# A feed-forward in two phases, with the down product as seven block products

## The reference, cut to what matters

```python
def swiglu(x, w_gate, w_up, w_down):
    return (jax.nn.silu(x @ w_gate) * (x @ w_up)) @ w_down
```

## Time and profile before

| what | value |
|---|---|
| median of 3 timed runs | 1898.8 us (1897.58 to 1910.72) |
| span of the profiled execution, first to last instruction | 1893.8 us |
| TensorE busy | 1788.9 us |
| VectorE busy | 843.5 us |
| ScalarE busy | 413.6 us |
| GpSimd busy | 57.5 us |
| read from memory | 230.07 MB |

### The profile page before, as it was taken

How to read it: one execution, slowest core, us unless ns; L and a number is a source line. 1 busy time by engine, 2 the same in 40 slices (tenths; PEclk the granted TensorE clock), 3 DMA queues, 4 the chain that set the end, 5 groups by cost and what they waited for, 6 DMA issues and landing times.

```text
span 1893.8 us, 25538 instructions
## 1 busy us (share of the span) xinstructions
PE 1788.9 (94%) x10478; PEld 1358.7 (72%) x10478; DVE 843.5 (45%) x1790; ACT 413.6 (22%) x1010; POOL 57.5 (3%) x71
## 2 busy tenths in 40 slices
PE   7999989999999999999988999899998999999997
PEld 5777768776587876878766778587886677556774
DVE  3244333744334335444357747434433444324353
ACT  1000022533200002000146412200002253113521
POOL 0200000000000000000003130000000000000000
PEclk9999998999999999999998959999998999999999
DMA  6754554212344544544433300254556762467520
GB/s 225 251 181 142 137 134 134 67 67 81 120 156 136 198 134 134 177 157 161 158 103 105 126 24 1 90 162 150 168 157 102 114 96 84 88 82 106 99 89 22
DMA packets 194168, 232.74 MB, mean 123 GB/s; under 512 B 27028, under 2 KB 175960, under 8 KB 194056
## 3 DMA queue, kind: packets, MB, share of 16 engines
q1 hardware_dynamic: 191584, 224.97, 43.3%
q0 software_dynamic: 1840, 5.12, 0.9%
q10 hardware_dynamic: 632, 1.04, 0.1%
HBM read 230.07 MB, written 1.05 MB: 122 GB/s over the span
## 4 chain that ended last, share of the span: by engine, by line
PE 89%; DVE 5%; ACT 2%; issue 2%; DMA 1%; ACTq 0%; DVEq 0%
PE ps L502 26%; PE ps L275 25%; PE ps L555 15%; PE ps L462 6%; PE ps L516 3%; PE ps L1629 1%; DMA ring<-in_ffn_w_up 1%; PE ps L1464 1%; PE ps L358 1%; PE ps L2148 1%; PE ps L2164 1%; PE ps L2152 1%; PE ps L2178 1%; PE ps L2183 1%; PE ps L1646 1%
## 5 line engine op out<-in xcount | busy, mean ns | idle before, releaser
L275 PE MATMUL ps<-hT,ring 128*128 128x272 f32 (+2 forms) x1504 | 363.9, 396 | 3.6 <-issue 1.3
L275 PEld LDWEIGHTS ps<-hT,ring 128*128 128x128 f32 (+1 forms) x1504 | 280.8, 190 | 65.2 <-issue 8.5
L555 PE MATMUL ps<-ring,arena 128*128 128x512 f32 x704 | 309.4, 592 | 0.0
L555 PEld LDWEIGHTS ps<-ring,arena 128*128 128x128 f32 x704 | 130.4, 190 | 147.3 <-issue 147.3
L502 PE MATMUL ps<-arena 128*128 128x128 f32 x1920 | 222.7, 276 | 0.0
L502 PEld LDWEIGHTS ps<-arena 128*128 128x128 f32 x1920 | 219.4, 193 | 0.0
L502 PEld LDWEIGHTS ps<-hT,ring 128*128 128x128 f32 x1280 | 156.8, 193 | 26.0 <-issue 19.1
L502 PE MATMUL ps<-hT,ring 128*128 128x128 f32 x1280 | 163.6, 276 | 6.4 <-DMA ring<-in_ffn_w_up 6.4
L627 DVE TENSOR_TENSOR arena<-arena,ps 128x256 f32<-128x256 f32 x40 | 16.8, 421 | 256.5 <-ACT arena L591 256.5
L640 DVE TENSOR_TENSOR arena<-arena,ps 128x384 f32<-128x384 f32 x80 | 44.2, 554 | 183.4 <-PE ps L502 183.4
L593 ACT ACTIVATE arena<-arena 128x512 f32<-128x512 f32 x40 | 25.2, 630 | 384.7 <-DVE arena L640 384.7
(11 more groups left out here) (408 smaller groups left out, 2165.7 us busy)
## 6 DMA issues: line engine op xcount, KB each, us to landing
ring<-in_ffn_w_gate SPq DMA_DIRECT2D x44, 1024.0 KB, 5.5
ring<-in_ffn_w_up SPq DMA_DIRECT2D x44, 1024.0 KB, 5.8
ring<-in_ffn_w_down SPq DMA_DIRECT2D x44, 1024.0 KB, 5.0
ring<-in_w_in SPq DMA_DIRECT2D x32, 1024.0 KB, 9.4
ring<-in_ab_w_in SPq DMA_DIRECT2D x12, 1024.0 KB, 5.3
ring<-in_w_out SPq DMA_DIRECT2D x8, 1024.0 KB, 5.0
ring<-in_ab_w_out SPq DMA_DIRECT2D x6, 1024.0 KB, 4.9
ring<-in_c_w_k SPq DMA_DIRECT2D x4, 1024.0 KB, 5.5
```

What stands on the lines that cost most here:

```text
L275: last = nc.tensor.matmul(o, l, r, start=(i == 0), stop=(i == len(pairs) - 1))
L555: m = nc.tensor.matmul(ps[:, 2 * t + h, :], hid[:, q % 2, i, t * P:(t + 1) * P], slot2(s0 + 3 * q + 2)[:, i, h * 512:(h + 1) * 512], start ...
```

## The change

The order of a feed-forward is now: gate and up of all 11 pairs, with all of `hid` kept in `arena` (11 x 512 columns), then the down product of all pairs. `plan_weights` lists all gate and up pieces first, then the 11 down pieces, and SP's loop is written out.

The down product of a pair is itself formed of seven block products, p1 to p7, of 128x512 each, gathered over the pairs in seven PSUM banks. VectorE makes four sums of weight blocks for every pair (`down_sums`) and four sums of blocks of `hid` for every four pairs (`hidden_sums`). Gate and up alternate between banks 4 to 7 and 0 to 3.

Behind it, VectorE adds the seven products to the four blocks of `y` (`y_blk`), Pool multiplies them by the gain (`trans_pool`), and ScalarE squares them from SBUF. Pool's clears for the mixer now wait for `x_new` and not for `hidden`.

```diff
         for q in range(NPAIR):
             plan.append([wide(g, 256 * q)])
             plan.append([wide(u, 256 * q)])
+        for q in range(NPAIR):
             plan.append([tall(dn, 2 * q)])
...
+            if post == 0.5:
+                c = dve_c()
+                p1, u2, u3, u4 = (y_part[:, i] for i in range(4))
...
+                dve.wait_ge(p1_out, c)
+                with_product(u2, p1, "p6").then_inc(y_step, 1)
+                with_product(y_blk[:, 0, 0], p1, "p2").then_inc(y_blk_in, 1)
+                dve.wait_ge(y_step, 3 * c - 2)
+                with_product(u4, u2, "p5").then_inc(y_step, 1)
+                dve.wait_ge(y_step, 3 * c - 1)
+                with_product(y_blk[:, 0, 1], u4, "p3").then_inc(y_blk_in, 1)
+                with_product(u3, u2, "p7").then_inc(y_step, 1)
+                dve.wait_ge(y_step, 3 * c)
+                with_product(y_blk[:, 1, 1], u3, "p5").then_inc(y_blk_in, 1)
+                with_product(y_blk[:, 1, 0], u3, "p4", ALU.subtract).then_inc(y_blk_in, 1)
+                for t in range(T):
+                    dve.wait_ge(y_sq, 2 * dve_sq())
+                    nc.vector.tensor_tensor(y_ms[:, t:t + 1], y_ss[:, 2 * t:2 * t + 1], y_ss[:, 2 * t + 1:2 * t + 2], ALU.add).then_inc(y_ms_in, 1)
+                    dve.wait_ge(y_root, dve_yr())
+                    dlink(dve, nc.vector.reciprocal(y_ms[:, t:t + 1], y_ms[:, t:t + 1]))
+                    dve.wait_ge(z_pool, 2 * dve_z())
+                    nc.vector.scalar_tensor_tensor(x[:, t, :], xn[:, t, :], y_ms[:, t:t + 1], x[:, t, :], ALU.mult, ALU.add).then_inc(x_new, 1)
...
+        def trans_pool(pool, gain):
+
+            for t in range(T):
+                for i in range(2):
+                    h = i if t == 0 else 1 - i
+                    c = slice(512 * h, 512 * h + 512)
+                    pool.wait_ge(y_blk_in, pool_b())
+                    nc.gpsimd.tensor_tensor(xn[:, t, c], y_blk[:, t, h], gains[:, gain, c], ALU.mult).then_inc(z_pool, 1)
...
+        P_BANK = {"p1": 4, "p6": 5, "p2": 6, "p5": 7, "p3": 0, "p7": 1, "p4": 2}
...
             def first_half(q):
-                n, u = s0 + 3 * q, 10 * call + q - 1
-                pe.wait_ge(a_taken, u)
+                n, u = s0 + 2 * q, 10 * call + q - 1
+                a = gu_a(q)
+                if q >= 3:
+                    pe.wait_ge(a_taken, u - 1)
...
+            def down(q):
+                slot, g, at_g = slot2(d0 + q), q // 4, q % 4
+                ts, ss = d_sum[:, q % 2], hid_sum[g][:, :, at_g]
+                sums_t, sums_s = 4 * (NPAIR * call + q), 4 * (3 * call + g)
...
+                take_slot(pe, d0 + q)
+                pe.wait_ge(hidden, c0 + q + 1)
+                if q == 0:
+                    pe.wait_ge(b_taken, 20 * call + 18)
+                m = one("p1", hid[:, q, 0, 0, :], slot[:, 0, 0:512])
...
+                pe.wait_ge(d_sums, sums_t + 3)
+                pe.wait_ge(hid_sums, sums_s + 3)
+                one("p6", ss[:, 1], ts[:, 1])
+                one("p2", hid[:, q, 1, 0, :], slot[:, 1, 0:512])
+                one("p5", ss[:, 0], ts[:, 0])
+                pe.wait_ge(hid_sums, sums_s + 4)
...
+                one("p3", ss[:, 3], slot[:, 1, 512:1024])
+                one("p7", ss[:, 2], ts[:, 2])
+                pe.wait_ge(d_sums, sums_t + 4)
+                if q == 0:
+                    pe.wait_ge(b_taken, 20 * call + 20)
+                m = one("p4", hid[:, q, 1, 1, :], ts[:, 3])
...
             direct()
             for q in range(1, NPAIR):
                 first_half(q)
...
+                second_half(q)
+            for q in range(NPAIR):
+                down(q)
...
                 if q < LAST:
                     weight_sums(dve, call, q + 1)
+                else:
+                    down_sums(dve, call, 0)
+                    down_sums(dve, call, 1)
...
+                if q == LAST - 1:
+                    hidden_sums(dve, call, 0)
+            hidden_sums(dve, call, 1)
+            for q in range(2, NPAIR):
+                down_sums(dve, call, q)
+                if q == 4:
+                    hidden_sums(dve, call, 2)
```

More of the change, by code:

```diff
@@ L304, in load_slot @@
                 sp.dma_start(dst, src).then_inc(slot_in[n % NSLOT], 16)
[L306 to L329, removed]
+        XN, SQ, XMN, SQM = arena[:, 16384:18432], arena[:, 0:1024], arena[0:META, 14336:15360], arena[0:META, 13312:14336]
         xn = XN.rearrange("p (t n) -> p t n", t=T)
@@ L533, in first_half @@
                         pe.wait_ge(w_sums, 8 * u + 2 * v + w + 1)
-                        first, m = product(gu_a[:, w, i], w_diff[:, q % 2, w, v], h_diff[:, v])
+                        first, m = product(a[:, w, i], w_diff[:, q % 2, w, v], h_diff[:, v])
                 m.then_inc(gu_half, 1)
             def second_half(q):
-                n, u = s0 + 3 * q, 10 * call + q - 1
+                n, u = s0 + 2 * q, 10 * call + q - 1
+                b = gu_b(q)
                 pe.wait_ge(h_sums, 4 * call + 4)
@@ L541, in second_half @@
                     pe.wait_ge(hidden, c0 + q)
-                else:
-                    pe.wait_ge(b_taken, 2 * u)
+                elif q >= 3:
+                    pe.wait_ge(b_taken, 2 * (u - 1))
                 for w in range(2):
-                    first, m = product(gu_b[:, w, 0], w_part(n + w, 0, 1), h_part(1, 0))
-                    if w == 1 and q < LAST:
+                    first, m = product(b[:, w, 0], w_part(n + w, 0, 1), h_part(1, 0))
+                    if w == 1:
                         first.then_inc(slot_used, 1)
@@ L548, in second_half, with one @@
                     pe.wait_ge(w_sums, 8 * u + 7 + w)
-                    product(gu_b[:, w, 1], w_diff[:, q % 2, w, 3], h_part(1, 1))
-                    first, m = product(gu_b[:, w, 2], w_part(n + w, 1, 1), h_diff[:, 3])
+                    product(b[:, w, 1], w_diff[:, q % 2, w, 3], h_part(1, 1))
+                    first, m = product(b[:, w, 2], w_part(n + w, 1, 1), h_diff[:, 3])
                     m.then_inc(gu_done, 1)
[L553 to L558, removed]
+            def down(q):
+                slot, g, at_g = slot2(d0 + q), q // 4, q % 4
+                ts, ss = d_sum[:, q % 2], hid_sum[g][:, :, at_g]
+                sums_t, sums_s = 4 * (NPAIR * call + q), 4 * (3 * call + g)
+                def one(name, left, right):
+                    m = nc.tensor.matmul(ps[:, P_BANK[name], :], left, right, start=(q == 0), stop=(q == LAST))
+                    if q == LAST:
+                        m.then_inc(p_done, 1)
+                    return m
+                take_slot(pe, d0 + q)
[4 more added lines that the diff above has]
+                if q == 0:
+                    m.then_inc(slot_used, 1)
+                pe.wait_ge(d_sums, sums_t + 3)
[4 more added lines that the diff above has]
+                pe.wait_ge(hid_sums, sums_s + 4)
+                if q == 0:
+                    pe.wait_ge(a_taken, 10 * call + 10)
+                one("p3", ss[:, 3], slot[:, 1, 512:1024])
+                one("p7", ss[:, 2], ts[:, 2])
+                pe.wait_ge(d_sums, sums_t + 4)
+                if q == 0:
+                    pe.wait_ge(b_taken, 20 * call + 20)
+                m = one("p4", hid[:, q, 1, 1, :], ts[:, 3])
+                if q < LAST:
+                    m.then_inc(slot_used, 1)
+                else:
+                    pe.drain().then_inc(slot_used, 1)
@@ L595, in weight_sums @@
         def weight_sums(dve, call, q):
-            n = at[("ffn", call)] + 3 * q
+            n = at[("ffn", call)] + 2 * q
             d_q = w_diff[:, q % 2]
@@ L1349, in mixer_pool @@
         def mixer_pool(pool):
-            pool.wait_ge(hidden, NPAIR)
+            pool.wait_ge(x_new, T)
             nc.gpsimd.memset(xpad[:, :, 0:3], 0.0).then_inc(m_zero, 1)
```

120 lines of the change are left out of this document (76 added, 44 removed).

## The result

The changed kernel takes **1880.3 us** (median of four runs, 1878.8 to 1882.1); the kernel before, beside it, takes 1898.6 (four runs). The ratio is 0.990 with a 95% interval of 0.986 to 0.993: faster, by 18 us. The forecast was 1861.6, with a range of 1850 to 1874. The direction was right, the size was half of what was forecast, and the time lies outside the range. It also lies, by 0.5 us, inside the band of 1% (1879.8 to 1917.8) that the prediction called hard to tell from no change and gave a chance of 0.06.

A forecast was written before the change was run, and what follows sets the result against it. The prediction took TensorE, busy 1788.9 of 1893.8 us, as the bound; -37.8 (down product) - 9.4 (stall) + 10.0 (ends) = -37.2 gave span 1856.6, plus 5.0 for the median, 1861.6 us; own range 1855 to 1868, with rivals 1850 to 1874.

The forecast's parts named there:

- Sum: Whole kernel: -37.8 - 9.4 + 10.0 = -37.2, span 1893.8 to 1856.6, plus 5.0 of median above span, 1861.6 us.
- Rival D: Ends of calls: longer TensorE gap, then records longer at half clock, up to 2.5 us more a call; 1871.6, chance 0.08.
- Part 1: Down product: seven matmuls a pair in place of eight, 44 pairs x 0.859 = 37.8 us less on TensorE.
- Part 2 and 3: Gate and up without the down product between them, and the border of the phases: VectorE's sums in time, cost 0.
- Part 4: Call 0: TensorE's stall for up weights goes as the ring runs three pairs ahead, 9.4 us less.
- rival B: Call 0: the stall for weights stays, 6.4 us and the clock after; -27.8, 1871.0 us, chance 0.13.
- Part 5: End of each call: longer chain of combinations, gain and x updates, 2.5 us times four, +10.0, ends 5.9 and 11.2.
- The 1.5 us of order: End of a call: row block 0 finished only after the combinations, transposes at E+5.95 instead of 4.48, four times +5.9.
- the lock: End of a call: VectorE's x update and Pool's multiplications exclude each other on SBUF; end costs 2.2 or 2.8, not 1.5.
- E: Down product: waits show at 308 single matmuls in changing banks, 0.1 us each, +31, 1892 us; chance 0.04.
- F: Gate and up: the ring starves the first phase, a pair takes 13.6, +44, time 1905.6 us; chance 0.05.
- C: Ends of calls: no exclusion between VectorE and Pool, the end costs 1.5; -41.3, 1857.5 us, chance 0.08.

The follow-up runs named there:

- b_wait1: The kernel before, with one VectorE clear of 128x1024 (about 0.9 us) put behind feed-forward call 2: 1922.8 us, one run.
- b_burst6: The kernel before, with six extra 128x512 matmuls, their result overwritten, just ahead of layer 1's recurrence: 1905.2 us, ten runs, ratio 1.000.

## Why the prediction was wrong, by its own steps

**The step that failed is the Sum**, where the span 1893.8 "becomes 1856.6" by terms of the feed-forward and its ends alone. It took for granted that all other stages keep their time. In place of nothing, the recurrence of layer 1 gave +19.9 us, all of it granted clock: 0.94 on average before, 0.50 after (19.3 over the whole stretch between the calls). The mixer of layer 0 gave another +2.6, of which 2.1 are the 32 records at a lower clock behind call 0. No rival held the 19.9. Rival D had records at half clock "up to 2.5 more a call", a small cost right behind the gap, and the 2.1 are of that kind, once and not four times; the clock that mattered failed to rise in a stage that begins some 180 us behind the end of call 2 and whose start the change had only shifted. The terms as measured, -37.8 - 9.4 + 10.8 + 2.6 + 19.3 = -14.5, make the span 1879.3, and it is 1879.4. On top the prediction put the 5.0 us by which the median of before lay above its profiled span; after, the median lies 0.9 above. That is an error of 4.1 the other way, so the span was missed by 22.8 us and the time by 18.7.

The trace of before held a warning: TensorE came to that stage at 0.50 and rose 3 us into it, in a stretch of 28.7 us that costs 48.6 if it does not rise. That stood as a possible +20 in a forecast whose whole gain was 37. The executions of the kernel before bear on it too: beside the last experiments five of 19 took 1919.8 to 1922.9 us at a mean clock of 0.952 to 0.954, all others but one 1895.6 to 1900.1 at about 0.965. That they lost the same 20 us in the same place is argued from size and clock; they left no trace. The trace of b_wait1, with the same time (1922.8) and mean clock (0.951), does show it there.

**Part 1, the down product, -37.8: held.** 66.1 us a call were foreseen (77 of these matmuls at 0.859), and the chain's piece of 65.25 for 152 records has the same 0.429 us each.

**Part 2 and 3, gate and up without cover, and the border, 0: held.** The pair takes 12.51 as before, and no window of a call holds over 0.1 us of idle TensorE. VectorE's spare time was enough for 34 us more work a call (88.8 to 123 busy).

**Part 4, the stall, -9.4: held, with less room than stated.** The load that decides was foreseen between 88.5 and 95.7; it was asked for at 68.82 and landed 24.2 us later, at 93.0. Need was put at 94.3 for TensorE and about 91 for VectorE, which did wait 1.85 us. The 5.8 us of slack that spoke against rival B was really 1.3 at TensorE (94.3 - 93.0). Pool's start was foreseen at 56.8 and was 56.60.

**Part 5, the ends, +10.0: the size held, the mechanism in part.** The four ends cost +3.05 and three times +2.6, 10.8 in all. The 1.5 us of order stood: 2.60 of gap, less the 0.69 and 0.45 that follow, is 1.46. (One reading under it was wrong: in the earlier trace rows the second multiplication, L412, waits for ScalarE's squaring and not for L410, so these rows did not show the spacing of dependent operations; the combinations end at E+1.2 as foreseen all the same.) Of the lock the prediction saw the x update (+0.45), and missed the addition of two sums of squares (+0.69), which starts while the third Pool multiplication runs. The Trainium skill, "SBUF — State Buffer", section "Who interferes with whom", covers both, since it speaks of any VectorE instruction with two SBUF inputs, and the trace agrees (0.84 against 0.15, 1.73 against 1.28); the prediction applied it only to the wide one. The end of call 0 has 0.44 more: Pool's three clears lie beside VectorE's scaling, which takes 1.19 us in place of 0.75. The prediction had put that at "at most 0.5".

**The rivals.** B, E and F did not occur. C (no lock, 1857.5) falls by the rows at the end of call 1. D's 1871.6 came nearest in number: its mechanism showed once, behind call 0, for 2.1 of the 22.8 us by which the span was missed.

## What to carry to other kernels

A change that shifts a stage by some us can turn the granted clock of a stage that it does not touch: before summing, look through the clock of every stage, and price at both levels each one that enters at 0.50. When a result disagrees with a sum whose terms all show up in the trace, put a delay of a few us and a short run of wide matmuls ahead of the suspect stage into both kernels, and compare those. And look for the smallest instructions in a dependent chain beside Pool, since they wait as long as the wide ones.

## What the hardware showed that had not been expected

- TensorE, continuously busy with small matmuls for 48.6 us, stayed at a granted clock of 0.50 (1.2 GHz) throughout; with the stage started 2.7 us later it rose to 1.00 (2.4 GHz) after some 3 us, and two starts 0.2 us apart rose after 4 and after 15 us. Wide 128x512 matmuls ahead of it (8.27 us of them in the changed kernel, 7.14 in the kernel before) were followed by 1.00 in both kernels, and none of the ten runs of b_burst6 was long (1902.7 to 1906.5). The Trainium skill, "TensorE: Matmul & The Clock Gate", section "What's actually happening", says that the point of transition varies by 500 ns either way, and that for modelling "the ramp penalty is <1% of a typical kernel span". That it varies agrees with these runs, but here by tens of us; the penalty was 19.9 us of 1879.4, 1.1%, and larger than what the change brought.
- A VectorE addition over 128x1 took 0.84 us instead of 0.15 because it started inside a Pool multiplication over 128x512 of 1.27 us: what it pays is about the other's remainder (0.69 here, 0.45 for the 128x1024 update in the next one), whatever its own size.
- A load of 1 MB that lands in 6.8 us took 24.2 beside the gains on the Pool queue. TensorE came to it 1.3 us after it had landed.
